# Unsplit latent queries, their last four units inside the expert pass, four units abreast at each norm, and a gate moved into the head norm

## The reference

```python
for l in range(2):
    h, hc = rms_norm(x, g1) * (1 + sc1) + sh1, ...     # modulated norm, latent and context
    lat, con = project_heads(h, w_in[l], rope), project_heads(hc, w_in[l], None)
    ya, yb, yc = mixers(lat, con)                      # yc then goes through diff_head_norm
    x = x + gt1 * ((sigmoid(h @ wga) * (ya @ wa) + sigmoid(h @ wgb) * (yb @ wb)
                    + sigmoid(h @ wgc) * (yc @ wc)) @ w_out)
    h2 = rms_norm(x, g2) * (1 + sc2) + sh2
    x = x + gt2 * peer_ffn(h2, wq, keys, u, v)
    # layer 0 does the same for the context tokens xc
return rms_norm(x, g_final)

def peer_ffn(t, wq, keys, u, v):                       # product-key expert retrieval
    q = (t @ wq) as 8 heads x 2 sides x 128
    s = q . keys; sv, si = top_k(s, 16) for each side; the best 16 of the 16 x 16 sums -> e, g
    return sum over the 8 x 16 chosen experts of g * gelu(u[e] . t) * v[e]
```

## Time and profile before

| | |
|---|---|
| median of 3 runs | 3136.88 us (3135.76 to 3145.63) |
| profiled execution | 3129.49 us, span 3127.7 us |
| PE / VectorE / ScalarE / POOL busy | 74% / 61% / 41% / 29% of the span |
| bytes moved | 1011.35 MB, mean 323 GB/s |
| of these, expert rows (queue of POOL) | 810.08 MB |

### The profile page before, as it was taken

One profiled execution on the slowest core, in us unless ns is written; L12 is line 12 of the kernel. 1 busy time (PEld: TensorE's weight loads), 2 busy tenths in 40 slices (PEclk: granted clock), 3 DMA queues, 4 the chain that ended last, 5 costly groups with the idle time before them and its releaser, 6 DMA issues.

```text
span 3127.7 us, 33640 instructions
## 1 busy us (share of the span) xinstructions
PE 2329.4 (74%) x11532; PEld 1355.8 (43%) x11532; DVE 1899.0 (61%) x4493; ACT 1266.7 (41%) x3385; POOL 891.6 (29%) x790
## 2 busy tenths in 40 slices
PE   5999998686679979665656788768998855555555
PEld 3787897343346636221211344237797611111111
DVE  3328646876865563686666544456854796666654
ACT  4216535346732333443324433245643534333333
POOL 0000000343433333443334443310000344444442
PEclk7999998888999989787777899879998977788777
DMA  5631243999999999999999999952143699999996
GB/s 237 248 128 36 103 159 140 417 387 392 388 387 398 406 421 410 389 419 421 404 421 400 396 421 421 422 219 107 45 177 124 261 419 421 421 421 421 417 420 289
DMA packets 139706, 1011.35 MB, mean 323 GB/s; under 512 B 15632, under 2 KB 15760, under 8 KB 17168
## 3 DMA queue, kind: packets, MB, share of 16 engines
q0 software_dynamic: 112032, 810.08, 63.3%
q1 hardware_dynamic: 27216, 196.45, 16.2%
q10 hardware_dynamic: 288, 2.69, 0.2%
HBM read 1008.10 MB, written 1.05 MB: 323 GB/s over the span
## 4 chain that ended last, share of the span: by engine, by line
PE 41%; DMA 31%; DVE 15%; ACT 7%; POOL 3%; issue 3%; ACTq 0%; POOLq 0%; DVEq 0%; SPq 0%
DMA att<-experts_in,att 30%; PE ps L1190 11%; DVE att L2348 6%; PE ps L604 5%; PE ps L605 5%; PE ps L606 5%; PE ps L1085 4%; POOL att L1764 3%; DVE ring_lo L1810 2%; ACT wt_hi L1286 2%; PE ps L889 2%; PE ps L855 1%; ACT att L1573 1%; PE ps L867 1%; PE ps L986 1%
## 5 line engine op out<-in xcount | busy, mean ns | idle before, releaser
L1190 PE MATMUL ps<-att 128*64 128x512 f32 x3072 | 978.9, 772 | 673.8 <-ACT att L1573 673.7
L1764 POOL DMA_INDIRECT att<-experts_in,att x768 | 881.2, 1147 | 1767.7 <-PE ps L1190 1113.8
L2348 DVE CUSTOM_DVE_ANT_0 att<-att 128x1024 f32<-128x1024 f32 x768 | 930.8, 1224 | 615.4 <-DMA att<-experts_in,att 611.5
L1190 PEld LDWEIGHTS ps<-att 128*64 128x64 f32 x3072 | 224.4, 163 | 1320.3 <-ACT att L1573 983.3
L1566 ACT ACTIVATE att<-att 128x1 f32<-128x1 f32 x768 | 153.9, 200 | 943.4 <-DVE att L2348 942.1
L1810 DVE TENSOR_TENSOR ring_lo<-ring,wt_hi 128x2048 fp32r<-128x2048 f32 x84 | 192.4, 2292 | 291.2 <-ACT wt_hi L1286 291.1
L1573 ACT ACTIVATE att<-const,att 128x64 f32<-128x64 f32 x768 | 267.0, 348 | 72.0 <-ACT att L1568 1.8
L1568 ACT ACTIVATE att<-att 128x1 f32<-128x1 f32 x768 | 226.2, 294 | 24.9
L1286 ACT ACTIVATE wt_hi<-ring 128x2048 fp32r<-128x2048 f32 x84 | 160.3, 1909 | 176.5 <-PE ps L606 102.8
L604 PE MATMUL ps<-h,wt_hi 128*128 128x256 f32 (+1 forms) x616 | 196.8, 319 | 28.7 <-DVE h L1824 22.0
L605 PE MATMUL ps<-h,wt_hi 128*128 128x256 f32 (+1 forms) x616 | 189.1, 307 | 0.0
(11 more groups left out here) (247 smaller groups left out, 3511.7 us busy)
## 6 DMA issues: line engine op xcount, KB each, us to landing
ring<-stream_in SPq DMA_DIRECT2D x183, 1024.0 KB, 7.9
att<-experts_in,att POOLq DMA_INDIRECT x768, 12.5
att<-bias_in POOLq DMA_DIRECT2D x16, 256.0 KB, 3.0
x<-x_in ACTq DMA_DIRECT2D x1, 2048.0 KB, 8.5
att<-stream_in SPq DMA_DIRECT2D x2, 1024.0 KB, 6.9
spare<-stream_in SPq DMA_DIRECT2D x1, 1024.0 KB, 9.6
out<-att SPq DMA_DIRECT2D x1, 1024.0 KB, 3.9
const<-const_in ACTq DMA_DIRECT2D x1, 576.0 KB, 4.5
```

The costliest lines, as they stand in the source:

```text
L1190: last = mm(ps[HALF * s:HALF * (s + 1), d, :], diag[:, (m + s) % DIAGS, :], rows[:, (m + s) % SLOTS, D + 512 * d:D + 512 * (d + 1)], start ...
L1764: nc.gpsimd.indirect_dma_start(out=rows[:, m % SLOTS, :], out_offset=None, in_=experts_in, in_offset=bass.IndirectOffsetOnAxis(ap=index[:, ...
L2348: v.tensor_tensor_reduce(out=u_row, in0=u_row, in1=dup[:, n // HK, n % 2, :], scale=1.0, scalar=0.0, op0=ALU.mult, op1=ALU.add, accum_out= ...
```

## The change

- The pairs of the latent expert queries (`WQ_AT[0]`, `WQ_AT[2]`) are raw: h2 is one float32 tile in `spare`, made by `norm_plain`, and the 12 + 4 units are single fp32 matmuls. The keys of all three passes lie in `spare` too, and POOL's three waits are gone.
- Of the 16 units, PE does 4 abreast by chunk of h2, then 8 one after another, all before the expert pass. Units 12 to 15 and the key tiles (0,2) to (1,3) are `wq_rest`, seven ticks at slots 1 to 13 of `gather(0)` and `gather(2)`.
- In `proj_both` and `proj(CTX_1)`, too, the first four units go abreast by chunk; the second dense pair is therefore split before h is made in `proj_both`, and the first one earlier.
- `head_norm` of PE does gate item 0 of the merge between the sums and the spreads.
- The merge's stage splits two pairs fewer behind `w_out`.

Core of the diff (PE unless said otherwise):

```diff
-PICK_UNIT = 12
+WQ_FIRST, WQ_REST = 4, 12
+REST_UNIT_TICKS = 16 - WQ_REST + 3
+TOKENS_AT = [spread(1, (REST_UNIT_TICKS, 13)) + spread(20, ...), ..., spread(1, (REST_UNIT_TICKS, 13)) + spread(HK + 4, ...)]
-    WQ_AT.append(run(WQ_PAIRS, "dense"))
+    WQ_AT.append(run(WQ_PAIRS, "raw"))
-        keys_r = [words(14336, 16 * KEYS), spare[:, PAIR:2 * PAIR], words(14336, 16 * KEYS)]
+        keys_r = [spare[:, PAIR:2 * PAIR], spare[:, PAIR:2 * PAIR], spare[:, PAIR:2 * PAIR]]
 # proj_both; proj(CTX_1) alike, with raw ring order and banks 2 to 5
+                for c in range(DC):
+                    pe.wait_ge(h_ready, c + 1)
+                    for k in range(ABREAST):
+                        if c == 0 and k % 2 == 0:
+                            wait_dense(after(p0, k // 2))
+                        last = mm3(ps[:, k, 0:N_LAT], dense_slot(p0, k * DC + c), h(c, slice(0, N_LAT)), c == 0, c == DC - 1)
+                        if c == DC - 1:
+                            last.then_inc(proj_done, 1)
+                between(0)
+                between(1)
 # head_norm
                 last.then_inc(cn_sum, 1)
+                merge_item(l, 0)
                 for h in range(4):
                     pe.wait_ge(head_diag_ready, 4 * i + h + 1)
 # wq
+                for c in range(DC):
+                    pe.wait_ge(h_ready, (1, 3, 6)[r] * DC + c + 1)
+                    for u in range(WQ_FIRST):
+                        ...
+                        last = mm(ps[:, pq_bank(r, u), 0:N_LAT], raw_slot(p0, u * DC + c), h2_plain[:, c, :], ...)
+                for u in range(WQ_FIRST, WQ_REST):
+                    wq_unit(r, u)
+                    if 0 <= u - TOK_UNIT < 4:
+                        spread_tokens(r, u - TOK_UNIT, [(h2_plain, ident)])
+                    if u % 4 == 0:
+                        key_tile(r, 0, u // 4 - 1)
+                pe.wait_ge(pq_copied, 16 * r + WQ_REST)
+            def wq_rest(r):
+                pe.wait_ge(tok_copied, 4 * r + 4)
+                for u in range(WQ_REST, 16):
+                    wq_unit(r, u)
+                    if u == WQ_REST:
+                        key_tile(r, 0, 2)
+                    yield
+                for tiles in ([(0, 3), (1, 0)], [(1, 1), (1, 2)], [(1, 3)]):
+                    for tt, g in tiles:
+                        key_tile(r, tt, g)
+                    yield
 # ScalarE
-                for j in range(WOUT_PAIRS):
+                for j in range(WOUT_PAIRS - 2):
                     split(dense(WOUT_AT[i]) + j + 2)
+                for u in range(WQ_REST):                # wq
+                    copy_query(r, u)
+                    if 0 <= u - TOK_UNIT < 4:
+                        copy_tokens(r, u - TOK_UNIT)
+                pick_exps(r, 0)
+            def wq_rest(r):
+                yield
+                for u in range(WQ_REST, 16):
+                    copy_query(r, u)
+                    yield
+                yield from idle(2)
 # POOL, gather
-                    if n == 5 and r != 1:
-                        pool.wait_ge(tok_done, 4 * (r + 1))
-                        pool.wait_ge(pq_done, 16 * (r + 1))
-                    if n == SLOTS - 1 and r != 1:
-                        pool.wait_ge(keys_done, 8 * (r + 1))
 # VectorE, in place of wq_and_picks with its six splits
+            def first_picks(r):
+                at_once(sides_of(r, 0, 0))
+                at_once(picks_of(r, PASSES[r][0], 0))
+                at_once(sides_of(r, 0, 1))
+            split(dense(QKV_AT[0]))                     # start of the launch; ScalarE alike
             modulation(0, 1, 1, range(0, 2))
-            split(dense(QKV_AT[0]))
+            split(dense(QKV_AT[0]) + 1)
             at_once(scale_shift(0, gains[0][0], [0, 1], h1_0))
-            split(dense(QKV_AT[0]) + 1)
```

More of the change, by code:

```diff
@@ L904, in attention, with merge_item @@
                 values(len(steps) - 1)
+            def merge_item(l, item):
+                n, i = N_LAT, 2 * l
+                p0 = MERGE_AT[i]
+                branch = item % 6 // 2
+                if 4 <= item < 8:
+                    pe.wait_ge(cn_ready, 4 * i + item - 3)
+                if item >= 8:
+                    pe.wait_ge(prod_done, 3 * DC * i + (item - 8) // 2 + 1)
+                if item in (1, 3, 5):
+                    pe.wait_ge(y_lo_ready, 12 * l + 4 * (branch + 1))
+                if item == 0 and l == 1:
+                    pe.wait_ge(lat_lo_ready, 1)
+                count = DC if item % 2 == 0 else 4
+                for c in range(count):
+                    b = MERGE_BLOCK[item] + c
+                    if b % BLOCKS == 0:
+                        wait_dense(p0 + b // BLOCKS)
+                    if item % 2 == 0:
+                        src = [half[:, c, 0:n] for half in h1[l]]
+                    else:
+                        src = [half[:, 4 * branch + c, :] for half in ys[l]]
+                    last = mm3(ps[:, item % 8, 0:n], dense_slot(p0, b), src, c == 0, c == count - 1)
+                last.then_inc(merge_done, 1)
             def head_norm(l):
@@ L918, in head_norm @@
                        start=True, stop=True).then_inc(head_spread, 1)
[L920 to L944, removed]
             def w_out(l):
@@ L1139, in wq_plain, with wq_unit @@
                 yield
+            def wq_unit(r, u):
+                p0 = WQ_AT[r]
+                if u % 2 == 0:
+                    wait_pair(pe, p0 + u // 2)
+                pe.wait_ge(pq_copied, 16 * r + (u - 3 if u < WQ_FIRST + 2 else u - 1))
+                for c in range(DC):
+                    last = mm(ps[:, pq_bank(r, u), 0:N_LAT], raw_slot(p0, u * DC + c), h2_plain[:, c, :],
+                              start=(c == 0), stop=(c == DC - 1))
+                last.then_inc(pq_done, 1)
@@ L1251, in _ @@
             head_norm(0)
-            merge(0)
+            for item in range(1, 6 * DC):
+                merge_item(0, item)
             w_out(0)
             at_once(sums(1))
-            at_once(wq(0))
+            wq(0)
             gather(0, idle(REST_TICKS), behind_lat())
@@ L1262, in _ @@
             head_norm(1)
-            merge(1)
+            for item in range(1, 6 * DC):
+                merge_item(1, item)
             w_out(1)
             at_once(sums(6))
-            at_once(wq(2))
-            gather(2, idle(REST_TICKS), update(2, 0))
+            wq(2)
+            gather(2, idle(REST_TICKS), behind_last())
             at_once(update(2, 1))
@@ L2371, in update, with behind_last @@
                 yield
+            def behind_last():
+                yield from idle(REST_UNIT_TICKS)
+                yield from update(2, 0)
             def behind_lat():
+                yield from idle(REST_UNIT_TICKS)
                 yield from norm_plain(2, gains[0][0], 1)
@@ L2425, in _ @@
             merge(1)
-            at_once(norm(6, gains[1][1], [0], h2))
-            wq_and_picks(2)
-            gather(2, rest_of_picks(2), update(2, 0))
+            at_once(norm_plain(6, gains[1][1], 0))
+            first_picks(2)
+            gather(2, rest_of_picks(2), behind_last())
             at_once(update(2, 1))
```

127 lines of the change are left out of this document (57 added, 70 removed).

## The result

The changed kernel takes 3117.7 us (median of four runs, 3114.0 to 3121.6) where the kernel before takes 3136.3 beside it: ratio 0.9939, with a 95% interval of 0.9921 to 0.9957. A second series gave 3119.1 against 3138.0, ratio 0.9939 again. The forecast was 3121. The profiled execution took 3117.2 us, its span 3115.4: 12.3 less than before, while the medians are 18.6 apart.

A forecast was written before the change was run, and what follows sets the result against it. No one engine was taken to bound the launch (PE 41% of the chain, DMA 31%, VectorE 15%). Terms 5.2 + 7 + 4.8 + 1.5 - 2.5 = 16.0 us off the 3136.9 median gave 3120.9; range 3104 to 3137.

The forecast's parts named there:

- Head norm: Both layers: gate item 0 fills PE's wait, so item 1 starts 2.6 us earlier in each; 5.2 us gained.
- Behind w_out and the head of pass 0: Fewer splits start query scaling 5.5 us earlier; with the ninth gather earlier and rows in early, 7 us gained in all.
- the account of rows: Pass heads: counts rows landed before and after, crediting early ones as saved DMA time; 2.9 rows, 7 us, in pass 0.
- The rival named for this: Pass heads: early rows are worth only the first dot's lead, 3.3 us at each head; 3126 us; chance 0.14.
- Head of pass 2: Same stage as in pass 0, but no stream pair displaced and 4.5 us of gaps; 4.8 us gained.
- Context projection: Layer 1: units abreast free their buffers late, PE idles about 4 us before unit 4, then half clock; 2.5 us lost.
- First projection: Unit 1 ends 3.4 us earlier abreast, but PE idles and half clock takes back 2; 1.5 us gained.
- Both early splits fit, so h is no later: First projection: first split lies in a wait for modulation, second where the first was; no delay of h.
- The slower rival: Heads of the passes: waits between units keep PE at 1.2 GHz, 27 us lost a pass; 3175 us; chance 0.07.

The follow-up runs named there:

- e11: The changed kernel itself, unedited, run and profiled once more to see the scatter between executions; median 3119.1 us.
- e1: The changed kernel with the first four latent query units run one after another again, still unsplit; 3123.2 us.
- e8: The changed kernel with the sixth to eighth gathers of the first and third pass issued only behind the first dot; 3116.8 us.
- e4: The changed kernel with the second group of sides searched before the gates, and the first picks' exponentials put behind the ninth unit's copy and tokens; 3101.4 us.
- e9: As e4, but only ten latent query units ahead of the pass and six in its first slots; 3104.5 us.
- e5: The changed kernel with the key units of layer 1's context projection run one after another again, early splits kept; 3117.8 us.
- e12: The kernel before with the first two latent query pairs split within the norm, not ahead of the updates of x; 3140.8 us against 3140.0.

## Why the prediction was right

**Head norm**, 5.2 forecast: measured 3.8 + 1.2 = 5.0 in the first profile, but 0.1 + 1.4 = 1.5 in the second (e11), where the clock fell in both layers. The mechanism was right and VectorE was not last; that the sum came out at 5.0 is partly luck, as layer 0 gave more than 2.6 at full clock and layer 1 less, for the clock.

**Behind w_out and the head of pass 0**, 7 forecast: A + B + C is 7.6 shorter. But the way there was not the forecast's. The norm gained 7.3, not 5.5, since the sums followed the last update in 4.7 us. The units ahead of the pass ended at 532.9; the forecast, less the 3.1 us that the stage started earlier, says 537.1. Of these 4.2 us, 1.8 are the earlier norm (PE started at 483.56, for 485.4), 0.7 the four units abreast (16.2 us for 16.9; the half clock at their head was there, 0.50 until 488), and 1.7 the eight units after them at 3.45 us instead of 3.65 (ScalarE's copies in e1 are 3.45 apart where nothing lies between). So the ninth gather came 11.9 us earlier counted from w_out, and 4.2 of it were lost until the 33rd. In C DMA moved as many bytes as before, 26.15 MB (2.10 of them the two stream pairs of units 12 to 15) for 26.19, but at a mean of 394 GB/s for 422: the loss is the gap from 550 to 560, at 245 GB/s.

**The step that failed** is the account of rows: that three rows in early are "work done in a DMA-bound pass". Holding them back (e8) changed neither B, C nor D. Its sum, 2.9 rows or 7 us, came out right by luck: the ninth gather, earlier than forecast, made up for rows that were worth nothing. The rival named for this (3.3 at each head) had the rule right and the price wrong: it is the ninth gather that counts, as long as PE has room behind it (e4, and e9 for its limit), and it moved by more than the first dot was thought to.

**Head of pass 2**, 4.8: 5.5 and 7.7 (D, two profiles), with the same failed account of rows behind it. **Context projection**, -2.5: -1.8 and -1.5, by the pause forecast, 3.88 us; e5 undid it. The Trainium skill, "TensorE: Matmul & The Clock Gate", the section on the HAM clock gate, has activity release the throttle and idleness bring it back. The trace agrees: 1.00 was granted from 2092 to 2100, where dense work went on, and 0.72 from 2100 to 2106, with the pause in it.

**First projection**, +1.5: -0.7 and -1.7 (the head sums' reciprocal at 336.8 and 337.9, before at 336.1), not seen in the time. "Both early splits fit, so h is no later" was wrong: the second pair lands only at 47.4, behind the first split's old place, and h waits for it. The slot of unit 1 is free 1.7 us sooner, not 3.4, and the load into it takes 1.9 us longer, so unit 4 stays where it was, behind a pause of 7.65 us where 4 to 5 were forecast.

**The slower rival** (half clock in the slots) did not come: 550 to 570 is at 1.00, and so is 2460 to 2480 in pass 2.

The terms add up: 5.0 + 7.6 + 5.5 - 0.7 - 1.8 = 15.6, for 16.0 forecast. But other stretches took back 3.3 us, 2.6 of them between the 33rd gather of pass 0 and the norm of the context projection, so the first profile is only 12.3 us shorter than that of before. In the second the same terms give 1.5 + 7.0 + 7.7 - 1.7 - 1.5 = 13.0, that stretch takes back 7.1, and the profile is 6.3 us shorter. The medians fell by 18.6 and 18.9. So the forecast of the median is borne out by many runs, but its sum is not confirmed term by term to better than some microseconds.

## What to carry to other kernels

Taking work off the path pays where it is the work that the next stage's first element waits for: four units moved by one line were worth 15 to 18 us, while an earlier norm whose splits only moved behind it (e12), earlier rows (e8) and units abreast (e1) gave nothing up to that element or behind it. Then look at every other engine that idles ahead of that same element: using VectorE's wait of 15 us, and moving ScalarE's exponentials up in its list, was worth nearly as much again (e4). Work put into a wait should be priced at the slow clock too: here the clock fell in the gate of layer 1 in nine profiles of eleven.

## What was not expected of the hardware

The same program's clock falls or holds in one place from one execution to the next, with nothing in the program to tell them apart. The head norm's gate ran at 0.12 or 0.21 us a matmul in the two profiles of the changed kernel, which moved the second by 3.7 us. The pairs of picks around 864 to 890 ran at 3.68 us in both of these, and partly at 1.94 in the kernel before and in e8, whose code is the same there. Rows 80 to 128 scatter by 10 us over the kernels; that the clock does this too is not shown. From the 33rd gather to the context norm of layer 1 the profiles of the kernels with unsplit queries took 1464 to 1477 us, those of before and of e12 1461. Both of these were executions that ended below their kernel's median (3129.5 against 3138, 3133 against 3141), so this is either their luck or a cost of the change in these passes; which of the two stays open. If it is luck, it explains why the profiles are 12 us apart and the medians 19.
